# Hybrid decoder layer on one core: modulation sums moved to VectorE, early expert slots, and the branch stage reordered

## What is computed

```python
cs = silu(c)
mod = cs @ w_ada + b_ada                       # six parts: sh1, sc1, gt1, sh2, sc2, gt2
h = rmsnorm(x, norm1) * (1 + sc1) + sh1
da_q, da_k, da_v, ml_qk, ml_v, ml_o, ml_if, g_a, g_m = split(h @ w_in)
y_a = diff_attention(...)                      # 4 heads, ALiBi, causal, rmsnorm per head
y_m = rmsnorm(sigmoid(ml_o) * mlstm(...))      # 4 heads
merged = sigmoid(g_a) * (y_a @ w_br_a) + sigmoid(g_m) * (y_m @ w_br_m)
x = x + gt1 * (merged @ w_out)
h2 = rmsnorm(x, norm2) * (1 + sc2) + sh2
x = x + gt2 * hier_moe(h2, ...)                # 32 experts of width 256, top 2 in one group
out = rmsnorm(x, norm_f)
```

## Time and profile before

| | |
|---|---|
| median of 3 runs | 473.31 us (473.29 to 476.85) |
| profiled execution | 474.18 us, span 472.4 us |
| mean granted TensorE clock | 0.958 |
| busy share of the span: PE, PEld | 84%, 65% |
| busy share: DVE, ACT, POOL | 36%, 39%, 33% |
| DMA | 164.32 MB, mean 348 GB/s |

### The profile page before, as it was taken

One profiled execution on the slowest core, in us unless ns is written; L12 is line 12 of the kernel. 1 busy time (PEld: TensorE's weight loads), 2 busy tenths in 40 slices (PEclk: granted clock), 3 DMA queues, 4 the chain that ended last, 5 costly groups with the idle time before them and its releaser, 6 DMA issues.

```text
span 472.4 us, 8608 instructions
## 1 busy us (share of the span) xinstructions
PE 397.8 (84%) x3612; PEld 307.9 (65%) x3612; DVE 170.2 (36%) x351; ACT 186.4 (39%) x343; POOL 157.2 (33%) x125
## 2 busy tenths in 40 slices
PE   4399999999899899999999889889877396682963
PEld 4299999987879899997986536445444162440621
DVE  1898166798016540465235130312111103011023
ACT  3477457564694294543355122131212012030122
POOL 0499866758447449997400000000000000000000
PEclk9689999998999999999999999999999789798899
DMA  8999997379969256578999979999999999999942
GB/s 335 421 417 425 418 422 268 110 239 384 400 240 388 89 205 242 179 268 345 422 420 422 393 294 422 420 420 421 422 420 422 420 422 420 420 420 422 420 186 91
DMA packets 23513, 164.32 MB, mean 348 GB/s; under 512 B 2608, under 2 KB 2736, under 8 KB 4656
## 3 DMA queue, kind: packets, MB, share of 16 engines
q1 hardware_dynamic: 23040, 162.15, 84.6%
q10 hardware_dynamic: 432, 1.57, 0.9%
HBM read 162.67 MB, written 1.05 MB: 347 GB/s over the span
## 4 chain that ended last, share of the span: by engine, by line
PE 66%; DMA 20%; DVE 5%; ACT 4%; issue 3%; SPq 2%; DVEq 0%; ACTq 0%
PE bank L1329 17%; DMA ring<-in_e 12%; PE cs_b L1669 9%; PE cs_b L1329 9%; DMA gm<-in_e 6%; PE bank L1372 5%; PE bank L1635 5%; PE bank L1680 4%; PE bank L1624 3%; PE cs_b L1282 3%; PE bank L1377 3%; SPq L441 2%; DMA const<-in_const 1%; DMA ring<-in_rest 1%; PE cs_b L1624 1%
## 5 line engine op out<-in xcount | busy, mean ns | idle before, releaser
L483 POOL TENSOR_TENSOR ring_r<-ring,his_r 128x512 fp32r<-128x512 f32 x120 | 156.8, 1345 | 60.3 <-ACT his_r L506 60.3
L741 ACT ACTIVATE raw<-bank,sm 128x128 f32<-128x128 f32 x72 | 27.2, 458 | 149.7 <-PE bank L1635 149.7
L506 ACT ACTIVATE his_r<-ring 128x2048 fp32r<-128x2048 f32 (+1 forms) x32 | 57.6, 1801 | 27.5 <-DMA ring<-in_rest 14.0
L1669 PE MATMUL cs_b<-ring,raw 128*32 128x256 f32 x544 | 50.6, 398 | 8.9 <-DMA ring<-in_e 8.9
L1207 DVE TENSOR_TENSOR tmp<-cs_b,tmp 128x256 f32<-128x256 f32 x8 | 3.4, 425 | 135.1 <-ACT tmp L749 135.1
L1669 PEld LDWEIGHTS cs_b<-ring,raw 128*32 128x32 f32 x544 | 26.5, 115 | 23.7 <-issue 13.4
L1635 PEld LDWEIGHTS bank<-const,xn 128*128 128x128 f32 x288 | 34.1, 191 | 9.2 <-issue 6.7
L1635 PE MATMUL bank<-const,xn 128*128 128x128 f32 x288 | 35.8, 277 | 1.7 <-DVE const L1199 1.7
L1329 PE MATMUL bank<-his_r 128*128 128x256 f32 x208 | 29.8, 286 | 0.0
L1329 PEld LDWEIGHTS bank<-his_r 128*128 128x128 f32 x208 | 26.6, 190 | 1.4 <-issue 1.4
L1624 PE MATMUL bank<-v,const 128*128 128x512 f32 x54 | 24.7, 594 | 3.0 <-issue 3.0
(11 more groups left out here) (391 smaller groups left out, 811.2 us busy)
## 6 DMA issues: line engine op xcount, KB each, us to landing
ring<-in_e SPq DMA_DIRECT2D x48, 1024.0 KB, 26.0
ring<-in_rest SPq DMA_DIRECT2D x40, 1024.0 KB, 8.5
his<-in_e SPq DMA_DIRECT2D x17, 1024.0 KB, 26.3
ring<-in_block SPq DMA_DIRECT2D x8, 768.0 KB, 20.0
late<-in_e SPq DMA_DIRECT2D x5, 1024.0 KB, 22.8
qkT<-in_e SPq DMA_DIRECT2D x5, 1024.0 KB, 26.1
mqk<-in_e SPq DMA_DIRECT2D x5, 1024.0 KB, 26.3
gm<-in_e SPq DMA_DIRECT2D x4, 1024.0 KB, 22.5
```

The lines of the kernel that those rows point to most:

```text
L483: pool.tensor_tensor(ring_r[:, slot_of(n), sl], ring[:, slot_of(n), sl], hi(d)[:, sl].bitcast(F32), ALU.subtract).then_inc(s["w_lo"], 1)
L506: act.activation(hi(d)[:, 0:WIDTH[d]], ring[:, slot_of(n), 0:WIDTH[d]], ACT.Copy).then_inc(s["w_hi"], 1)
L741: ins = act.activation(xg[:, b, k, :], source[:, j * P:(j + 1) * P], ACT.Identity, bias=S("B2", KD)[:, k:k + 1], scale=S("A2", KD)[:, k:k ...
L1669: ins = pe.matmul(up_bank[e * CAP:(e + 1) * CAP, half], xg[:, b, k, e * CAP:(e + 1) * CAP], wt[e][:, k, :], start=(k == 0), stop=(k == KD ...
```

## The change

- Parts 3, 4, 2 and 5 of the modulation leave TensorE. Their units now hold 256 transposed columns of `w_ada`, and VectorE's `sums_of(i, u)` does two sums over 1024 for each of 16 units, at places of its list between other work. Their slots are spent when the sum is done. gt1 and gt2 are spread with `gate_rows` on TensorE, and their bias DMAs go.
- The units of the modulation stand at other places of `UNITS`, mostly two or three between gates.
- Three of the 21 expert slots (`home` twice, and a half of `o_att`) are loaded early, among the units; x is loaded behind `ymT1` into `late`.
- Banks recur every six jobs, since `cs_b` stays in use; from wo2 on there are eight again.
- The Silu of q and k comes ahead of the output gates on ScalarE; gates and splits interleave with the rest in a new order; TensorE's projections too.
- `y` is no more written twice: the low part reads the bank (`y_low`), and the merge works in PSUM (`merge`), `merged_low` reads it there. wo0 waits for the last of these.
- The constants are loaded ahead of xT. `w_r` is scaled by one instruction. `norm_f` is loaded by SP late.

```diff
-    units += w_in(C_MQK, 4) + w_in(C_MV, 2) + ada(3) + w_in(C_MO, 1) + ada(4) + w_in(C_MO + 256, 1)
-    units += w_in(C_GA, 1) + ada(2) + w_in(C_GA + 256, 3) + w_in(C_GM, 4)
-    units += [("br_a", 0), ("br_a", 512), ("br_m", 0), ("br_m", 512)] + ada(5)
+    units += w_in(C_MQK, 4) + w_in(C_MV, 2) + w_in(C_MO, 2) + w_in(C_GA, 2)
+    units += ada((3, 0), (3, 1), (3, 2)) + w_in(C_GA + 512, 1) + ada((3, 3), (4, 0)) + w_in(C_GA + 768, 1)
+    units += ada((4, 1), (4, 2)) + w_in(C_GM, 1) + ada((4, 3), (2, 0)) + w_in(C_GM + 256, 2) + ada((2, 1), (2, 2))
+    units += w_in(C_GM + 768, 1) + ada((2, 3), (5, 0)) + [("br_a", 0)] + ada((5, 1), (5, 2), (5, 3)) + [("br_a", 512)]
+    units += [("br_m", 0), ("br_m", 512)]
...
+EARLY = {NFIRST + 9: (0,), NFIRST + 18: (1,), NFIRST + 20: (2,)}
...
+            if kind == "ada":
+                return s["sums"], ADA.index(n) + 1
...
+            sp.dma_start(const[:, 0:NFRONT], t["const"][:, 0:NFRONT]).then_inc(const_in, 16)
             sp.dma_start(hT[:].rearrange("p k n -> p (k n)"), t["xT"]).then_inc(xT_in, 16)
-            sp.dma_start(const[:, 0:NFRONT], t["const"][:, 0:NFRONT]).then_inc(const_in, 16)
...
+            def sums_of(i, u):
+
+                n = UNITS.index(("ada", (i, u)))
+                dve.wait_ge(landed[slot_of(n)], landed_value(n))
+                for a in range(2):
+                    w, at = slot(slot_of(n))[:, a * D:(a + 1) * D], 8 * (i - 2) + 2 * u + a
+                    ins = dve.tensor_tensor_reduce(w, w, cs_b[:], 1.0, 0.0, ALU.mult, ALU.add, m2[:, at:at + 1])
+                ins.then_inc(s["sums"], 1)
+                dve.wait_ge(s["sums"], ADA.index(n) + 1)
...
-            for k in range(KD):
-                dve.tensor_scalar(w_r[:, k, :], w_r[:, k, :], A2[:, k:k + 1], None, ALU.mult).then_inc(s["wr_r"], 1)
+            sums_of(4, 1)
+            sums_of(4, 2)
...
+            def merge(i):
+
+                job = f"brm{i}"
+                both_sides = pb(job)[:].rearrange("p (a n) -> p a n", a=2)
                 dve.wait_ge(*free(f"gm{i}"))
                 dve.wait_ge(*full(job))
-                release(dve.tensor_tensor(view, pb(job)[:].rearrange("p (a n) -> p a n", a=2), view, ALU.mult), job)
-                dve.wait_ge(*free(job))
-                own(dve.tensor_tensor(va, va, view, ALU.add), "merged", i + 1)
+                link(dve.tensor_tensor(both_sides, both_sides, gm2[:, 2 * i:2 * i + 2, :], ALU.mult))
+                dve.wait_ge(*free(f"bra{i}"))
+                own(dve.tensor_tensor(both_sides, both_sides, ga[:, 2 * i:2 * i + 2, :], ALU.add), "merged", i + 1)
...
+            branch("a", 1)
+            branch("m", 0)
+            branch("m", 1)
+            gate_rows(1, 0)
+            gate_rows(1, 1)
             pe.wait_ge(s["m_hi"], 4)
-            merged_src = (lambda k: merged_hi[:, k, :], lambda k: merged_lo[:, k, :], ((s["m_lo"], 4),))
+            pe.wait_ge(*free("brm3"))
+            merged_src = (lambda k: merged_hi[:, k, :], lambda k: merged_lo[:, k, :], (free("brm3"),))
```

More of the change, by code:

```diff
@@ L55, in unit_list, with ada @@
 def unit_list():
-    def ada(i):
-        return [("ada", (i, k)) for k in range(0, KD, 2)]
+    def ada(*parts):
+        return [("ada", part) for part in parts]
     def w_in(c0, n):
@@ L71, in unit_jobs @@
 def unit_jobs():
[L73 to L76, removed]
+    jobs = [f"ml{i}" for i in range(4)] + ["mv0", "mv1", "mo0", "mo1"] + [f"ga{i}" for i in range(4)]
+    jobs += [f"gm{i}" for i in range(4)] + ["bra1", "bra3", "brm1", "brm3"] + [f"wo{i}" for i in range(4)]
+    jobs = iter(jobs)
+    return [None if kind in ("mod", "block", "ada") else next(jobs) for kind, _ in UNITS]
 UNITS = unit_list()
@@ L81 @@
 NFIRST = 2 * KD
+ADA = [n for n, (kind, _) in enumerate(UNITS) if kind == "ada"]
 DENSE = [n for n, (kind, _) in enumerate(UNITS) if kind not in ("ada", "mod")]
@@ L97 @@
 FIRST_JOBS = ([("ss", 0), ("cs0", 6), ("cs1", 7)] + [(f"qk{i}", i) for i in range(4)] + [("v0", 4), ("v1", 5)])
[L98 to L103, removed]
+JOBS = (["if", "ml0", "s0", "s1", "ml1", "s2", "s3", "ml2", "s4", "s5", "ml3", "s6", "s7", "ifT", "mv0", "mv1", "mo0", "mo1",
+         "ga0", "aT0", "aT1", "cols", "Mb0", "Mb1", "ga1", "o0", "o1", "aT2", "aT3", "ga2", "ga3", "rb", "ms0", "ms1",
+         "gm0", "num0", "ms2", "num1", "ms3", "gm1", "num2", "num3", "gm2", "yaT0", "yaT1", "gm3", "bra0", "bra1",
+         "ymT0", "ymT1", "bra2", "bra3"] + [f"brm{i}" for i in range(4)] + ["gt1b0", "gt1b1"])
+TAIL = (("wo0", None), ("wo1", None), ("wo2", 6), ("x2T0", 7), ("x2T1", None), ("wo3", None), ("x2T2", None), ("lg", None),
+        ("x2T3", None), ("rank", 7), ("gt2b0", None), ("g1", 6), ("gt2b1", 7))
 UNIT_JOB = unit_jobs()
@@ L594, in _ @@
             scale(3)
+            for i in range(4):
+                act.wait_ge(*free(f"ml{i}"))
+                pair = mqk[:, 2 * i:2 * i + 2, :].rearrange("p a n -> p (a n)")
+                act.activation(pair, pair, ACT.Silu).then_inc(s["mqk_r"], 1)
             output_gate(0)
             split(17)
+            output_gate(1)
+            split(18)
             def copy_a(h):
@@ L677, in _ @@
[L677 to L688 removed]
+            gate(gm2, "gm", 2)
@@ new lines, in _, with y_high @@
+            split(25)
+            def y_high(name, i):
+                act.wait_ge(*full(f"y{name}T{i}"))
+                k = 2 * i + (4 if name == "m" else 0)
+                act.activation(yT_hi[:, k:k + 2, :], pb(f"y{name}T{i}")[:].rearrange("p (a n) -> p a n", a=2), ACT.Identity,
+                               scale=S("dgain", 1) if name == "a" else col("mlstm_norm"), bias=0.0).then_inc(s["y_hi"], 1)
+            y_high("a", 0)
+            y_high("a", 1)
+            gate(gm2, "gm", 3)
@@ L953, in _ @@
             mix(1)
-            rows(3)
             gate_sums()
@@ L978, in _ @@
                 decay_arg(h)
-            rows(4)
-            columns(A2, 4)
-            own(dve.scalar_tensor_tensor(out=A2, in0=A2, scalar=1.0, in1=col("norm2", 0, 8),
-                                         op0=ALU.add, op1=ALU.mult), "mod2", 2)
-            rows(2)
+            for u in range(4):
+                sums_of(3, u)
+            columns(B2, 3).then_inc(s["mod2"], 1)
+            sums_of(4, 0)
             dve.wait_ge(s["h_sq"], 1)
@@ L1093, in residual @@
                 own(dve.tensor_tensor(xv, xv, tv, ALU.add), "x2", i + 1)
-            rows(5)
+            spread(gt1b, 1)
+            dve.wait_ge(*free("gt1b1"))
             for i in range(4):
@@ L1457, in _ @@
                 filled(ins, f"Mb{i}")
-            ada(4)
-            proj("mo1", hsrc, next_dense(8))
+            proj_T("ga1", hsrc, next_dense(8))
             pe.wait_ge(*free("v0"))
```

387 lines of the change are left out of this document (187 added, 200 removed).

## The result

| | before | after |
|---|---|---|
| median | 474.02 us (17 runs, 472.69 to 478.4) | 477.27 us (17 runs, 475.48 to 480.63) |
| ratio | | 1.0061, 95% interval 1.0042 to 1.0080 |
| profiled execution | 474.18 us, span 472.4 | 480.63 us, span 478.8 |
| granted clock in it | 0.958 | 0.924 |

The account below looks back on a forecast made before the run. The prediction took the first expert product's start as bound, set by TensorE's job list with its waits. wo0 6.7 us earlier, less 2.0 clock, plus 2.4 start, gave 7.1: 467.1, as median 466.2 us; range 455.5 to 471.

Parts of the forecast that it names:

- the start: Constants loaded ahead of xT bring TensorE's first pass 2.4 us earlier, with bounds 0 and 3.
- the wait in front of rb: TensorE stands 6.3 us before rb, because ScalarE's squares of o queue behind its split of late-landing gm1.
- its queue: gm1's load stands behind gm0, ada(4,3), the third early expert and ada(2,0), at 2.49 us each: home at 140.7.
- the wait in front of bra0: bra3's unit lands late, its split precedes y_high, and TensorE loses 2.2 us more before bra0.
- early loads that do not show: Three early expert loads leave the time unchanged, since the queue resumes with slots of the first quad's second product.
- The distance from first expert product to end: Fixed at 214.9 us, plus 1.8 around the span, if the 21 early loads are home by then.
- the walk from mo1 to ga1: TensorE's jobs in sequence: mo1 ends at 111.3, ga0 at 117.3, small jobs at 120.2, ga1 at 126.0.
- a rival at 1.7 us: No change, chance 0.15: ga1 and wo0 start at half clock and the start gives only 1; 471 us.
- The clock behind the stand: Half clock after TensorE's 6.3 us idle before rb: 2.0 us taken, at most 3 lost.
- VectorE in front of wo0: From 193.1, sums, two gated_a, small ones, merges and low parts end at 210.9; wo0 starts at 211.0.
- The rival in which sums are stretched by GpSimd: VectorE's 14 sum instructions before wo0 each wait nearly 1 us more; wo0 14 us later, 480 us; chance 0.07.
- the rival in which the cover holds: gm1 and bra3's unit arrive in time, both TensorE waits vanish: 19.3 us gained, 454 to 455 us; chance 0.20.

Follow-up runs that it names:

- run 1: Kernel before, with only the constants loaded ahead of xT and VectorE's two small instructions on them ahead of its squares: 471.37 us, ratio 0.9946.
- run 2: Kernel after, with ScalarE's split of gm1 moved behind the squares and root of o: 468.0 us, ratio 0.9879 to the kernel before.
- run 4: Kernel after, with the third early expert load issued behind gm1's load instead of two units ahead: 474.74 us, ratio 1.0003 to the kernel before.
- run 9: Kernel after, with gm1's split behind the squares of o and bra3's split behind the high parts of y_a: 463.68 us, ratio 0.9783.
- run 12: Kernel after with four orders changed (two splits, reciprocal, gate 2 columns) and no early expert loads: 459.78 us, ratio 0.9710 to the kernel before.
- run 5: Kernel after, with VectorE's reciprocal for the last attention head ahead of the five decay-sum instructions: 476.71 us, ratio 1.0061 to the kernel before.
- run 3: Kernel after, with TensorE computing ga3 twice to stay busy in the gap before rb: 478.44 us, ratio 1.0069 to the kernel before.
- runs 7 and 8: Kernel after with gate 2's 8-column addition moved behind the last low part: 477.52 us, ratio 1.0085; and kernel after repeated unchanged: 477.94 us.

## Why the prediction was wrong

The walk down to the first expert product, its times less the 2.4 us of the start and with the 2.0 of clock from gm0 on:

| | forecast | after | late by |
|---|---|---|---|
| ga0 ends | 114.9 | 116.2 | 1.3 |
| decay's small jobs end | 117.8 | 119.8 | 2.0 |
| ga1 ends | 123.6 | 129.7 | 6.1 |
| gm0's split (its landing) | 128.3 | 135.4 | 7.1 |
| gm1's split (its landing) | 138.3 | 145.3 | 7.0 |
| rb starts | 144.8 | 151.8 | 7.0 |
| gm0 ends | 155.5 | 164.9 | 9.4 |
| bra0 starts | 179.8 | 189.5 | 9.7 |
| brm3 ends | 204.6 | 214.7 | 10.1 |
| wo0 starts | 210.6 | 222.0 | 11.4 |
| first expert product | 250.4 | 263.8 | 13.4 |
| end, with 215 and 1.8 | 467.1 | 480.6 | 13.5 |

- **Right, and shown by taking them away:** the start (2.4 us, run 1); the wait in front of rb, with the chain from gm1's split on (6.3 forecast, 6.75 measured, run 2); its queue, 2.49 us a unit (run 4); the wait in front of bra0 (2.2 and 2.4, run 9); early loads that do not show (run 12). The distance from first expert product to end kept within 0.1 us in the pair of profiles; in the variants it was 214.7 to 217.6, so "fixed" holds to some 3 us only, and a microsecond won ahead of it is not always a microsecond of time.
- **The term that failed first** is the walk from mo1 to ga1: "mo0, mo1 end at 111.3, ga0 at 117.3, small jobs to 120.2, ga1 126.0". I let these jobs follow each other without any wait, at their durations of before. Measured are 1.7 us of waits for low parts (0.41, 0.57, 0.69), 0.3 for an output gate, 2.0 for the bank that the gate of ga0 frees, and 2.2 for the first half of ga1 at half clock (121.79 to 126.87 for three groups that take 2.87 elsewhere): 6.2 us, against 6.1 in the table. ScalarE was late there because its Silu and output gates were behind the 7.3 us wait of run 5. From ga1's end the delay goes on through SP's list: gm0's load waits for that end, and gm1's is issued behind it. gm0's split started 5.65 us after ga1's end, where I had 4.75, and gm1's 9.9 us after gm0's, as forecast (4 x 2.49). So gm1 landed 7.0 us late. That I had half clock at ga1 in a rival at 1.7 us, and not in the sum, was a choice on the wrong side. In run 5's trace the wait for the bank and the half clock are gone, one low part is 1.3 later, and 3.0 of the 6.1 us come back in all. The other waits were not taken away one by one.
- **The clock behind the stand** was mis-sized: 2.0 in the sum, by a range that I bounded at 3 us from one stretch. The same jobs took 13.1 us behind the stand and 8.8 without it: 4.3. In front of wo0 it came too (4.53 us for three groups, 1.7 lost), which I had put in the range and not in the sum. It came once more in the routing stage (the 128x512 products of L1627 took 5.4 us, 3.8 before), where I had nothing. The Trainium skill, page "TensorE: Matmul & The Clock Gate", section "HAM oscillation — how this bites in real kernels", describes waits of 3 to 5 us for data, each of which throws the array back to its lower clock; run 3, where the idleness is mostly filled, agrees for this kernel (1.97 us for rb instead of 3.63).
- **VectorE in front of wo0:** the list from y_low m was forecast at 17.8 us, and it took 20.1 us (201.8 to 221.9). Everything in it came at its price except the 8-column addition, part of "small ones 0.4", which took 3.4 in both profiles of after. That the timed executions pay it too is not shown (runs 7 and 8). The rival in which sums are stretched by GpSimd had the right neighbour and the wrong instruction: the sums took 1.215 us on average, as forecast; some instructions with both inputs in SBUF were stretched. The ground that I gave for the sums was thinner than I wrote: of the four in the earlier trace rows the first two ran beside GpSimd, which then stood idle from 20.1 to 23.2 us.
- **The direction.** Forecast was 19.3 us gained if every cover held, less 12 for three waits and the clock, and a gain of 7 was left. The same kind of error, small and of one sign, came at five places (the walk to ga1, gm0's landing, and the clock behind the stand, at wo0 and in the routing stage), with the addition as a sixth in the profile, and took 11 us median to median. No rival had it, since the slower one was a single mechanism on the sums; the range ended at 471.

So the 16.3 us of products that left TensorE were not a false gain. They were spent on waits, two of which were only a matter of which line stands first in ScalarE's list: with those moved the kernel is at 463.7 us, and at 459.8 to 462.0 with the other edits, 2.7 to 2.9% faster than before, at or just above the upper end of the rival in which the cover holds (454 to 460).

## What to carry to other kernels

When work leaves the bounding engine, list for every engine beside it the first instruction that waits for a landing, and what stands behind that instruction in the same list: a copy of weights that are needed 6 us later must not stand ahead of a reduction that frees a bank now. Do the same for the engine that issues the loads: a load can go out only when the slots of all loads ahead of it in the list are free (here 12.7 us of waiting for one job). Price an idle gap of several microseconds on TensorE as the gap and a stretch at 1.2 GHz behind it (here 6.8 and 4.3 us). And a saving that is computed as "before, less what is removed" needs its small waits added: this list of jobs had 5.9 us of them before and 20.1 after.

## What was not expected of the hardware

- A VectorE addition of 128x8 took 3.38, 3.42, 3.55 and 4.01 us beside back-to-back GpSimd low parts of 1.3 us each, as long as two to three of them. At the same place, beside the same low parts, it took 0.17 us in the kernel of run 5 and 0.92 in that of run 2. What decides is not shown.
- TensorE computing 48 products for nothing in a gap of 6.8 us made the next 16 small ones 1.66 us shorter (3.63 to 1.97, one execution each).
- The load of a unit into an empty queue took 4.8 us from issue to split in one trace (181.31 to 186.11) and 6.6 in another (178.98 to 185.55), with nothing else queued. The cause is open.
- A stand of 4.3 us (run 4) left the 16 products of rb as slow as one of 6.75 us did: 3.58 and 3.63 us.
